# mLSTM heads in row form: denominators and norm factors as full rows, the spread of m behind the preceding head's last products

## The chip, the cores and the metric

The kernel runs on one core of a Trainium2 chip. The metric is the device time of one execution in microseconds (us). Only the engines of that one core are used: TensorE (PE; PEld is its weight load), VectorE (DVE), ScalarE (ACT), GpSimd (POOL) and SyncE (SP), which issues the weight loads.

## The reference

Two transformer blocks run one behind the other on 512 tokens of width 1024. The change touches only the mLSTM branch of the first one. The reference computes it in chunks with a running state; the kernel uses the equivalent form over the whole sequence. With F the running sum of the log forget gates, c = log i − F, M the running maximum of c (from 0) and m = F + M, each of the four heads of width 256 does:

```python
scores = (q @ k.T) / 16 * exp(c[s] - M[t])         # for s <= t, else 0
num = scores @ v
den = scores.sum(over s)
h = num / max(|den|, exp(-m))[:, None]
h = (h - mean(h)) * rsqrt(mean((h - mean(h))**2) + 1e-5)   # layer norm over the head's 256 columns
out = sigmoid(o) * h * head_g
```

Behind it come the gates with the second branch, the output projection and the rest of the two blocks.

## The kernel before

**Layout.** Activations lie transposed: features on the 128 partitions, the 512 tokens along the free axis. Every precise product is split: an fp32 operand becomes a high part in float32r (ScalarE, `xh`, `wh`) and the remainder (VectorE, `xl`, `wl`), and `mm3` issues three float32r products, high x high, high x low, low x high. A product of two fp32 operands that are not split is issued as one fp32 matmul, which shows as two records.

**Weights.** They stream as 312 units of 128x1024 through three buffers. In the plan, `("split", u)` makes SyncE fetch unit u + 3, ScalarE copy unit u to `wh` and VectorE subtract to `wl`; it stands two units ahead of TensorE's use.

**Order.** `make_plan()` writes one list of steps by hand; every engine walks through it in order and does its own part of each step, with semaphores between the engines. The projections ("pair" steps) give TensorE steady work; the steps of the heads are placed between them by tables. `MIX_AT[(u, kk)]` names the short steps that follow pair step kk of unit u. `H0.7` is step 7 of head 0's attention, `T0.7` step 7 of its norm. `GATE_AT` does the same for the gates (`Q`), the norm of the second branch (`L`) and its spatial products (`V`). The evacuation of the q and k projections (`qkev`: bias, three more taps of the convolution, silu, split) and that of the output gates (`ogev`) follow the last pair step of their units.

**Steps of a head** (before). H.0: TensorE spreads row M of head h over all partitions, by an fp32 product of `sel[:, h, :]` (4 rows, ones in row h) and `rows[:, 2, :]`, into PSUM bank 2. H.1, H.2: ScalarE takes exp(c − M), GpSimd masks the diagonal blocks. H.3: q k products. H.4: scores on VectorE. H.5, H.6: the split of the scores into `sh` and `sl`. H.7: TensorE makes the denominators as columns: for each block of 128 tokens, products of the scores (as weights) with two columns of ones, 20 in all, then the numerators, 24 products; ScalarE takes the absolute value of the 128x4 denominators, VectorE copies half of the numerator, takes the maximum with exp(−m) (which lies in `ccol` from gate step 4) and the reciprocal. T.0, T.1: the sum over the 256 columns by a product with ones; T.2: subtraction of the mean; T.3, T.4: squares; T.5: column sums of the squares (`col_sums`, four fp32 products with one column each); T.6: four VectorE operations and a Sqrt on 128x4 numbers give one factor for each token; T.7: VectorE puts them on the diagonals of a 128x512 tile; T.8: TensorE spreads these over all partitions (fp32, 512 columns); T.9: ScalarE copies the result; T.10: VectorE multiplies both halves of the head. `G` steps gate the heads' halves and add the second branch, on GpSimd for the first six.

**Gates.** `gmm` makes the gate rows, Q0 to Q2 compute log f, F, c, M and m in `rows`, Q3 transposes c and m on TensorE (eight small products), Q4 copies c and takes exp(−m) into `ccol`.

**Constants.** "mix" (GpSimd) builds `sel`; "ws" (VectorE) splits the spatial weights and scales the gates' weights, in the queue ahead of the diagonal of R, the factors of the mixing norm, whose product by TensorE stands within the next group of products.

Of the kernel before, what the change touches and what calls it, by code (L numbers as in the profile page):

```python
# [7 lines left out]
F32 = mybir.dt.float32  # L8
# [33 lines left out]
    (78, 3): "L15", (80, 1): "L16",  # L42
# [50 lines left out]
def short_steps(text):  # L93

    for w in text.split():
        name, _, seg = w.partition(".")
        c, n = name[0], name[1:]
        if c in "HT":
            yield (c, int(n), int(seg))
# [17 lines left out]
def make_plan():  # L117
# [247 lines left out]
def _build(nc, D, out, ctx):  # L365
# [50 lines left out]
    rows = sb("rows", [4, 4, 512], F32, mix)  # L416
    sel = sb("sel", [4, 4, 128], F32, mix)
# [182 lines left out]
    def three(f, p, plain, conv):  # L600
# [14 lines left out]
    mix_g = sig("s_mix_g", mix=lambda: ["sel0", "sel", "wm", "on4"])  # L615
# [6 lines left out]
                 gate=lambda i: {1: ["min", "F"], 2: ["c", "M", "m"], 4: ["cc"]}.get(i, []))  # L622
    gate_a = sig("s_gate_a", gate=lambda i: {0: ["abs", "exp", "ln"], 4: ["em"]}.get(i, []))
# [19 lines left out]
    h_p = sig("s_h_p", H=lambda h, s: {0: [(h, "M")], 3: [(h, "qk")], 7: [(h, "den"), (h, "num")]}.get(s, []))  # L643
    h_a = sig("s_h_a", H=lambda h, s: {1: [(h, "e", 0), (h, "e", 1)], 2: [(h, "e", 2), (h, "e", 3)],
                                       5: [(h, "s", 0), (h, "s", 1)], 7: [(h, "abs"), (h, "h0")]}.get(s, []))
    h_g = sig("s_h_g", H=lambda h, s: {1: [(h, 0), (h, 1)], 2: [(h, 2), (h, 3)]}.get(s, []))
    h_d = sig("s_h_d", H=lambda h, s: {4: [(h, "a", 0), (h, "a", 1)], 6: [(h, "l", 0), (h, "l", 1)],
                                       7: [(h, "h1"), (h, "max"), (h, "rec")]}.get(s, []))
    t_p = sig("s_t_p", T=lambda h, s: {1: [(h, "sum")], 5: [(h, "cs")], 8: [(h, "sp")]}.get(s, []))
    t_a = sig("s_t_a", T=lambda h, s: {3: [(h, "sq0")], 4: [(h, "sq1")], 6: [(h, "sqrt")], 9: [(h, "R")]}.get(s, []))  # L650
    t_d = sig("s_t_d", T=lambda h, s: {0: [(h, "add")], 2: [(h, "c0"), (h, "c1")], 4: [(h, "sq")],
                                       6: [(h, "v0"), (h, "v1"), (h, "rec"), (h, "v2")], 7: [(h, "diag")],
                                       10: [(h, "n0"), (h, "n1")]}.get(s, []))
# [102 lines left out]
    def _(e):  # L756
# [11 lines left out]
        for kind, *a in plan:  # L768
# [110 lines left out]
            elif kind == "gate":  # L879
                i, = a  # L880
                ra, rf = tmpm[0:4, 0, :], rows[:, 1, :]
# [7 lines left out]
                elif i == 4:  # L889
                    e.wait_ge(*gate_d.at("cc"))  # L890
                    act(ccol[:, 16:32], bank(6)[:, 16:32], ACT.Exp, scale=-1.0).then_inc(gate_a.sem, 1)
# [29 lines left out]
            elif kind == "H":  # L921
                h, s = a
                if s in (1, 2):
# [8 lines left out]
                elif s == 7:  # L932
                    e.wait_ge(*h_p.at(h, "den"))
                    act(rcs[:, h % 2, :], bank(2)[:, 0:8].rearrange("p (i z) -> p i z", z=2)[:, :, 0],
                        ACT.Abs).then_inc(h_a.sem, 1)
                    e.wait_ge(*h_p.at(h, "num"))
                    e.wait_ge(s_spill, 16)
                    act(hn[:, 2 * h, :], bank(0), ACT.Copy).then_inc(h_a.sem, 1)
            elif kind == "T":
# [145 lines left out]
    def _(e):  # L1085
# [9 lines left out]
        for kind, *a in plan:  # L1095
# [94 lines left out]
            elif kind == "ws":  # L1190
                e.wait_ge(*ws_a.at("h"))
                low(wsl[:, :], wsr[:, :], wsh[:, :]).then_inc(ws_d.sem, 1)
                for k in range(8):
                    e.tensor_scalar(wif[:, k, :], wif[:, k, :], col("gmix", k), None, ALU.mult).then_inc(ws_d.sem, 1)
            elif kind == "gmm":
                ri, rf = rows[:, 0, :], rows[:, 1, :]
# [9 lines left out]
            elif kind == "gate":  # L1206
                i, = a
                ri, rf, rM, rm = (rows[:, n, :] for n in range(4))
                if i == 1:
                    e.wait_ge(*gate_a.at("ln"))  # L1210
                    stt(rf, rf, 0.0, tmpm[0:4, 0, :], ALU.min, ALU.subtract).then_inc(gate_d.sem, 1)
# [10 lines left out]
                elif i == 4:  # L1222
                    e.wait_ge(*gate_p.at("tr"))
                    e.tensor_copy(ccol[:, 0:16], bank(6)[:, 0:16]).then_inc(gate_d.sem, 1)
            elif kind == "ln":
# [66 lines left out]
            elif kind == "H":  # L1292
# [11 lines left out]
                elif s == 7:  # L1304
                    cc = rcs[:, h % 2, :]
# [3 lines left out]
                    e.wait_ge(*h_a.at(h, "abs"))  # L1309
                    e.wait_ge(*gate_a.at("em"))  # L1310
# [905 lines left out]
```

## Time and profile before

| | us |
|---|---|
| median of three runs | 1939.83 (1939.72 to 1943.83) |
| profiled execution | 1945.08 |
| its span, first to last instruction | 1943.0 |
| TensorE busy | 1903.3 |
| VectorE busy | 1032.3 |
| ScalarE busy | 783.0 |
| GpSimd busy | 240.5 |

Times of rows are microseconds from the start of the span. The stretch in which the heads run goes from about 597 to 817 us. The busy time of TensorE includes the time in which it runs at a lower clock; the mean granted clock over the span is 0.988. A matmul's shown duration overlaps with that of the next one, so starts are to be compared. "x2" behind a row is the number of instructions merged in it.

### The profile page before, as it was taken

The numbers are of one execution on the slowest core, as the hardware profiler recorded it, in microseconds if no ns is written. First come the engines' busy times: TensorE is split into PE (matmuls) and PEld (weight loads), VectorE is DVE, ScalarE is ACT, GpSimd is POOL, SyncE is SP. The second block draws the span as 40 slices with busy tenths as digits, with TensorE's granted clock in tenths as the row PEclk, the third lists the DMA queues.
The fourth block names the chain that finished last, engine by engine and source line by source line (L and its number), as shares of the span: only waits on it lengthen the run. The fifth ranks groups of instructions, "written<-read, shape, count | busy, mean of one in ns | idle before, by whom it ended". The sixth has DMA issues, their size and how long they took to land.

```text
span 1943.0 us, 21345 instructions
## 1 busy us (share of the span) xinstructions
PE 1903.3 (98%) x8752; PEld 1571.7 (81%) x8752; DVE 1032.3 (53%) x1297; ACT 783.0 (40%) x1046; POOL 240.5 (12%) x264
## 2 busy tenths in 40 slices
PE   7999999999999999999999999999989999999997
PEld 5788888878888888888888888888877888888885
DVE  6444434347354666564444334655564877774345
ACT  4332322236443555433223222555554444443234
POOL 5000001201300111140000022100003100000212
PEclk9999999999999999999999999999989999999998
DMA  4423232342241222422222332312213232323331
GB/s 146 163 89 106 87 108 88 105 153 92 76 141 60 93 76 82 137 97 98 98 98 97 98 98 97 111 64 68 74 44 103 82 109 87 108 88 109 98 104 59
DMA packets 51074, 188.98 MB, mean 97 GB/s; under 512 B 6345, under 2 KB 6345, under 8 KB 50081
## 3 DMA queue, kind: packets, MB, share of 16 engines
q1 hardware_dynamic: 46224, 166.74, 26.0%
q0 software_dynamic: 4176, 19.83, 3.0%
q8 instruction: 69, 1.13, 0.2%
q10 hardware_dynamic: 576, 1.05, 0.1%
q14 instruction: 29, 0.23, 0.0%
HBM read 179.18 MB, written 11.03 MB: 98 GB/s over the span
## 4 chain that ended last, share of the span: by engine, by line
PE 95%; DVE 3%; ACT 1%; issue 0%; DMA 0%; DVEq 0%; ACTq 0%; POOLq 0%
PE psum L1675 95%; DVE xl L1090 1%; DVE wl L1093 1%; PE psum L2027 0%; DMA cols<-in_cols 0%; ACT at L766 0%; ACT wh L766 0%; DVE x L1087 0%; DVE az L1090 0%; DVE R L1125 0%; DVE at L1446 0%; DVE fta L1087 0%; DVE tm L1331 0%; ACT R L766 0%; DVE xl L1093 0%
## 5 line engine op out<-in xcount | busy, mean ns | idle before, releaser
L1675 PE MATMUL psum<-xh,wh 128*128 128x512 f32 x1760 | 697.1, 396 | 14.8 <-DVE xl L1090 11.6
L1675 PE MATMUL psum<-xl,wh 128*128 128x512 f32 x1760 | 687.7, 391 | 0.0
L1675 PE MATMUL psum<-xh,wl 128*128 128x512 f32 x1760 | 687.5, 391 | 0.0
L1093 DVE TENSOR_TENSOR wl<-wraw,wh 128x1024 fp32r<-128x1024 f32 (+1 forms) x313 | 405.4, 1303 | 388.1 <-ACT wh L766 387.5
L766 ACT ACTIVATE wh<-wraw 128x1024 fp32r<-128x1024 f32 (+1 forms) x313 | 325.7, 1050 | 382.1 <-PE psum L1675 380.1
L1675 PEld LDWEIGHTS psum<-xh,wh 128*128 128x128 f32 x1760 | 332.1, 189 | 94.5 <-issue 22.6
L1675 PEld LDWEIGHTS psum<-xl,wh 128*128 128x128 f32 x1760 | 332.1, 189 | 70.1 <-issue 2.9
L1675 PEld LDWEIGHTS psum<-xh,wl 128*128 128x128 f32 x1760 | 331.9, 189 | 70.1
L1539 POOL TENSOR_TENSOR ssq<-x 128x512 f32<-128x512 f32 x6 | 6.2, 1039 | 717.3 <-DVE x L1173 454.0
L1675 PE MATMUL psum<-wh,xh 128*128 128x512 f32 (+1 forms) x256 | 88.2, 344 | 0.4 <-ACT zv L766 0.4
L1675 PE MATMUL psum<-wh,xl 128*128 128x512 f32 (+1 forms) x256 | 86.0, 336 | 0.0
L1675 PE MATMUL psum<-wl,xh 128*128 128x512 f32 (+1 forms) x256 | 86.0, 336 | 0.0
L1675 PE MATMUL psum<-hha,wh 128*128 128x512 f32 x176 | 68.5, 389 | 0.0
L1675 PE MATMUL psum<-hla,wh 128*128 128x512 f32 x176 | 68.5, 389 | 0.0
L1675 PE MATMUL psum<-hha,wl 128*128 128x512 f32 x176 | 68.5, 389 | 0.0
L1675 PE MATMUL psum<-hhb,wh 128*128 128x512 f32 x176 | 68.5, 389 | 0.0
L1675 PE MATMUL psum<-hlb,wh 128*128 128x512 f32 x176 | 68.5, 389 | 0.0
L1675 PE MATMUL psum<-hhb,wl 128*128 128x512 f32 x176 | 68.5, 389 | 0.0
L1675 PE MATMUL psum<-hhc,wh 128*128 128x512 f32 x176 | 68.5, 389 | 0.0
L1675 PE MATMUL psum<-hlc,wh 128*128 128x512 f32 x176 | 68.5, 389 | 0.0
L1675 PE MATMUL psum<-hhc,wl 128*128 128x512 f32 x176 | 68.5, 389 | 0.0
L1090 DVE SCALAR_TENSOR_TENSOR ftc<-ftc,cols 128x511 f32<-128x511 f32 x88 | 64.1, 749 | 7.9 <-ACT ftc L766 6.4
(299 smaller groups left out, 2245.7 us busy)
## 6 DMA issues: line engine op xcount, KB each, us to landing
wraw<-in_w_ffn SPq DMA_DIRECT2D x87, 512.0 KB, 3.3
wraw<-in_w_down SPq DMA_DIRECT2D x44, 512.0 KB, 3.3
wraw<-in_w_up SPq DMA_DIRECT2D x44, 512.0 KB, 3.5
wraw<-in_w_qg SPq DMA_DIRECT2D x28, 512.0 KB, 3.3
wraw<-in_w_att SPq DMA_DIRECT2D x24, 512.0 KB, 3.3
wraw<-in_w_dn SPq DMA_DIRECT2D x22, 512.0 KB, 3.3
wraw<-in_w_zu SPq DMA_DIRECT2D x16, 512.0 KB, 3.3
wraw<-in_w_zv SPq DMA_DIRECT2D x8, 512.0 KB, 3.4
```

The lines of the kernel that those rows point to most:

```text
L766: return e.activation(dst, src, func, **kw)
L1090: return e.scalar_tensor_tensor(out=dst, in0=p, scalar=s, in1=q, op0=op0, op1=op1)
L1093: return e.tensor_tensor(dst, src, hi.bitcast(F32), ALU.subtract)
L1539: e.tensor_tensor(ssq[:, :], x[:, j, :], x[:, j, :], ALU.mult).then_inc(sq.sem, 1)
L1675: return e.matmul(dst, lhsT, rhs, start=start, stop=stop, skip_group_check=skip)
```

## The change

Denominators and norm factors stay rows that are alike on all partitions, so that nothing of them has to be turned from columns to rows.

- H.7: TensorE multiplies ones (128x128) with the scores, eight float32r products of 512, 384, 256 and 128 columns, which gives the denominator on all partitions. ScalarE squares it, scaled by 256e-5, into `tm(5)`; VectorE takes the maximum with 256e-5 exp(−2m), which becomes `em(h)` (in `ssg` or `R1`).
- A new step H.m: TensorE spreads row m over all partitions into bank 2, ScalarE takes exp(−2m) into `em(h)`. H0.m stands inside the second group of the v projection; the others stand 1.5 to 2 units or more ahead of their head's H.0, behind the preceding head's last products. H.0 now waits for that exponential.
- The spreads of M and m are float32r: `rowr` holds rows M and m, high parts on partitions 0 to 3 and remainders on 32 to 35, `sel` has 36 rows to match. A new gate step Q5 makes that split. "mix" and "ws" get a memset and four copies for zeros and ones.
- T.5: the sum of squares goes to all partitions by one fp32 product with ones, as in T.1. T.6: VectorE adds `em(h)`, ScalarE takes Ln and Exp(−0.5 ·). T.7 multiplies both halves. T.8 to T.10 are gone.
- The gates' transposes of m and their exponential are gone; gate rows move to `mg`.

```diff
-    (78, 3): "L15", (80, 1): "L16",
+    (78, 3): "L15 Q5", (80, 1): "L16",
...
+    (103, 1): "H0.7", (103, 2): "T0.0 H1.m", (103, 3): "T0.1", (104, 0): "T0.2", (105, 3): "T0.3 T0.4",
...
-    (109, 1): "H1.6", (110, 0): "T0.8", (110, 1): "H1.7 T0.9", (110, 3): "T0.10 G0 G1 T1.0", (111, 0): "T1.1",
-    (111, 1): "T1.2 T1.3", (111, 2): "T1.4", (111, 3): "T1.5", (112, 0): "T1.6", (114, 0): "H2.0 T1.7",
-    (114, 1): "H2.1 H2.2", (115, 2): "H2.3 T1.8 H2.4", (115, 3): "T1.9 H2.5", (116, 2): "T1.10 G2",
+    (109, 1): "H1.6", (110, 1): "H1.7", (110, 3): "G0 G1 T1.0", (111, 0): "T1.1",
+    (111, 1): "T1.2 T1.3", (111, 2): "T1.4 H2.m", (111, 3): "T1.5", (112, 0): "T1.6",
+    (114, 0): "H2.0 T1.7", (114, 1): "H2.1 H2.2", (115, 2): "H2.3 H2.4", (115, 3): "H2.5", (116, 2): "G2",
...
-    (119, 2): "T2.4", (119, 3): "T2.5", (120, 0): "T2.6", (122, 0): "H3.0 T2.7", (122, 1): "H3.1 H3.2",
+    (119, 2): "T2.4 H3.m", (119, 3): "T2.5", (120, 0): "T2.6", (122, 0): "H3.0 T2.7",
...
-        tgroup("v", c, 94 + 4 * c)
+        tgroup("v", c, 94 + 4 * c, {(1, 0, 3): (("H", 0, "m"),)} if c else None)
...
# ScalarE
+                if s == "m":
+                    e.wait_ge(*h_p.at(h, "m"))
+                    if h >= 2:
+                        e.wait_ge(*t_d.at(h - 2, "u"))
+                    act(em(h), bank(2), ACT.Exp, scale=-2.0).then_inc(h_a.sem, 1)
...
-                    act(rcs[:, h % 2, :], bank(2)[:, 0:8].rearrange("p (i z) -> p i z", z=2)[:, :, 0],
-                        ACT.Abs).then_inc(h_a.sem, 1)
+                    if h:
+                        e.wait_ge(*t_d.at(h - 1, "n1"))
+                    act(tm(5), bank(2), ACT.Square, scale=256e-5 ** 0.5).then_inc(h_a.sem, 1)
...
-                    act(c2, c2, ACT.Sqrt, bias=eps5[:, 0:1]).then_inc(t_a.sem, 1)
-                elif s == 9:
-                    e.wait_ge(*t_p.at(h, "sp"))
-                    act(tm(4), bank(7), ACT.Copy).then_inc(t_a.sem, 1)
+                    e.wait_ge(*t_d.at(h, "u"))
+                    act(tm(5), tm(5), ACT.Ln, scale=1.0 / 256).then_inc(t_a.sem, 1)
+                    e.wait_ge(*t_a.at(h, "ln"))
+                    act(tm(5), tm(5), ACT.Exp, scale=-0.5).then_inc(t_a.sem, 1)
...
# VectorE
+                e.wait_ge(*mix_g.at("zero"))
+                sel2 = sel[:, :, :].rearrange("p h t -> p (h t)")
+                e.tensor_copy(sel2, mg[0:36, 4, :]).then_inc(sel_d.sem, 1)
+                e.tensor_copy(rowr[:, :, :], mg[0:36, 4:6, :]).then_inc(sel_d.sem, 1)
+                e.wait_ge(*sel_d.at("zero"))
+                e.tensor_copy(sel2[0:4, :], mg[0:4, 3, :]).then_inc(sel_d.sem, 1)
+                e.tensor_copy(sel2[32:36, :], mg[0:4, 3, :]).then_inc(sel_d.sem, 1)
...
-                    e.tensor_tensor(cc, cc, ccol[:, 16:32].rearrange("p (i h) -> p i h", h=4)[:, :, h],
-                                    ALU.max).then_inc(h_d.sem, 1)
-                    e.wait_ge(*h_d.at(h, "max"))
-                    e.reciprocal(cc, cc).then_inc(h_d.sem, 1)
+                    e.wait_ge(*h_a.at(h, "em"))
+                    e.wait_ge(*h_a.at(h, "d"))
+                    stt(em(h), em(h), 256e-5, tm(5), ALU.mult, ALU.max).then_inc(h_d.sem, 1)
...
-                    stt(c2, bD[:, 0:4], 1.0 / 256, cc, ALU.mult, ALU.mult).then_inc(t_d.sem, 1)
...
+                    stt(tm(5), em(h), 3.0e38, bD, ALU.min, ALU.add).then_inc(t_d.sem, 1)
...
-                    e.tensor_tensor(quad(t4), eye4, wide(c2), ALU.mult).then_inc(t_d.sem, 1)
...
# TensorE
+                if s == "m":
                     if h:
-                        e.wait_ge(*h_a.at(h - 1, "abs"))
+                        e.wait_ge(*h_a.at(h - 1, "d"))
...
-                    mm(bank(2), sel[:, h, :], rows[:, 2, :]).then_inc(h_p.sem, 1)
+                    mm(bank(2), sel[:, h, :], rowr[:, 1, :]).then_inc(h_p.sem, 1)
+                elif s == 0:
+                    e.wait_ge(*h_a.at(h, "em"))
+                    mm(bank(2), sel[:, h, :], rowr[:, 0, :]).then_inc(h_p.sem, 1)
...
-                    for i in range(4):
-                        for j in range(i + 1):
-                            r = slice(OFF[j] + 128 * (i - j), OFF[j] + 128 * (i - j) + 128)
-                            mm(bD[:, 2 * i:2 * i + 2], sh[:, r], onesr[:, 0:2], j == 0, False)
-                            t = mm(bD[:, 2 * i:2 * i + 2], sl[:, r], onesr[:, 0:2], False, j == i)
+                    for j in range(4):
+                        r = slice(OFF[j], OFF[j] + 512 - 128 * j)
+                        mm(bank(2)[:, 128 * j:512], onesr[:, :], sh[:, r], j == 0, False)
+                        t = mm(bank(2)[:, 128 * j:512], onesr[:, :], sl[:, r], False, j == 3)
...
-                    col_sums(bank(7), tm(4)).then_inc(t_p.sem, 1)
-                elif s == 8:
-                    e.wait_ge(*t_d.at(h, "diag"))
                     mm(bank(7), ones[:, :], tm(4)).then_inc(t_p.sem, 1)
```

## Rows read from the trace of the kernel before

**Rows 1.** The page's first part: busy us, share of the span, instructions.

```profile
PE 1903.3 (98%) x8752; PEld 1571.7 (81%) x8752; DVE 1032.3 (53%) x1297; ACT 783.0 (40%) x1046; POOL 240.5 (12%) x264
```

**Rows 2.** Waits of TensorE, 560 to 830 us: total, times, longest.

```profile
PE psum L1675 <- DVE tm L1331: 0.6, 1, 0.6
```

**Rows 3.** TensorE by stretches: length, busy (instructions), granted clock, DMA share, GB/s.

```profile
612.02:615.40 3.38, 3.38 (x11) 0.50 0.00 0
...
721.25:724.65 3.40, 3.40 (x12) 0.50 0.44 177
...
779.25:782.70 3.45, 3.45 (x11) 0.51 0.70 209
```

**Rows 4.** Timeline of TensorE, head 0's step 7: start, us, instruction.

```profile
608.85 0.39 PE L1675 MATMUL psum<-xh,wl 128*128 128x512 f32 x1
609.08 0.17 PE L1675 MATMUL psum<-onesr,sh 128*128 128x2 f32 x1
...
611.22 0.49 PE L1675 MATMUL psum<-sh,vh 128*128 128x512 f32 x1
...
616.63 0.45 PE L1675 MATMUL psum<-xh,wh 128*128 128x512 f32 x1
```

**Rows 5.** Timeline of TensorE, head 1's numerators and what follows.

```profile
664.75 0.48 PE L1675 MATMUL psum<-sh,vh 128*128 128x512 f32 x1
...
668.59 0.45 PE L1675 MATMUL psum<-xh,wh 128*128 128x512 f32 x1
```

**Rows 6.** Timeline of TensorE around step T0.1.

```profile
619.21 0.39 PE L1675 MATMUL psum<-xh,wl 128*128 128x512 f32 x1
619.44 1.02 PE L1675 MATMUL psum<-tm,ones 128*128 128x512 f32 x2
...
620.76 0.40 PE L1675 MATMUL psum<-xh,wl 128*128 128x512 f32 x1
```

**Rows 7.** Timeline of TensorE on both sides of step T2.5.

```profile
737.32 0.39 PE L1675 MATMUL psum<-xh,wl 128*128 128x512 f32 x1
...
738.92 0.40 PE L1675 MATMUL psum<-xh,wl 128*128 128x512 f32 x1
```

**Rows 8.** Timeline of TensorE around step H0.0.

```profile
596.96 0.39 PE L1675 MATMUL psum<-xh,wl 128*128 128x512 f32 x1
597.27 1.12 PE L1675 MATMUL psum<-rows,sel 4*128 4x512 f32 x2
...
598.90 0.39 PE L1675 MATMUL psum<-xh,wl 128*128 128x512 f32 x1
```

**Rows 9.** Timeline of TensorE, one 64-row group of the attention stage.

```profile
1342.81 0.40 PE L1675 MATMUL psum<-xh,wl 128*128 128x512 f32 x1
1343.14 2.18 PE L1675 MATMUL psum<-aq 64*128 64x512 f32 x12
...
1345.82 0.40 PE L1675 MATMUL psum<-xh,wl 128*128 128x512 f32 x1
```

**Rows 10.** Timelines of VectorE and TensorE around the mixing norm's R.

```profile
408.91 0.69 DVE L1128 TENSOR_TENSOR R<-ident,rc 128x512 f32<-128x512 f32 x1
...
411.27 1.02 PE L1675 MATMUL psum<-R,ones 128*128 128x512 f32 x2
...
433.03 0.48 DVE L1203 TENSOR_SCALAR rows<-rows,bif 4x512 f32<-4x512 f32 x1
```

**Rows 11.** Timelines: a dependent ScalarE pair, then T1.6 to H2.3.

```profile
437.54 1.29 ACT L766 ACTIVATE tmpm<-tmpm 4x512 f32<-4x512 f32 x2
...
688.31 0.15 DVE L1090 SCALAR_TENSOR_TENSOR rcs<-psum,rcs 128x4 f32<-128x4 f32 x1
...
688.90 1.05 ACT L766 ACTIVATE wh<-wraw 128x1024 fp32r<-128x1024 f32 x1
...
698.60 0.69 DVE L1093 TENSOR_TENSOR qk<-tmpm,qk 128x512 fp32r<-128x512 f32 x1 [0.76 <-ACT qk L766]
...
701.17 1.07 PE L1675 MATMUL psum<-qk 128*128 128x512 f32 x4
```

More of the change, by code:

```diff
@@ L98, in short_steps @@
         if c in "HT":
-            yield (c, int(n), int(seg))
+            yield (c, int(n), seg if seg == "m" else int(seg))
         elif c == "S":
@@ L415, in _build @@
     vl = sb("vl", [128, 4, 1024], F32R, mix)
-    rows = sb("rows", [4, 4, 512], F32, mix)
-    sel = sb("sel", [4, 4, 128], F32, mix)
+    rows = sb("rows", [4, 2, 512], F32, mix)
+    rowr = sb("rowr", [36, 2, 512], F32R, mix)
+    sel = sb("sel", [36, 4, 128], F32R, mix)
     tmpm = sb("tmpm", [128, 4, 512], F32, mix)
@@ L497, in tm, with em @@
         return tmpm[:, i, :] if i < 4 else tm2[:, i - 4, :]
+    def em(h):
+        return (R1 if h % 2 else ssg)[:, :]
     def quad(ap):
@@ L621, in _build @@
     gate_d = sig("s_gate_d", gmm=lambda: ["i0", "f0", "i", "f"],
-                 gate=lambda i: {1: ["min", "F"], 2: ["c", "M", "m"], 4: ["cc"]}.get(i, []))
-    gate_a = sig("s_gate_a", gate=lambda i: {0: ["abs", "exp", "ln"], 4: ["em"]}.get(i, []))
+                 gate=lambda i: {1: ["min", "F"], 2: ["c", "M", "m"], 4: ["cc"], 5: ["rl"]}.get(i, []))
+    gate_a = sig("s_gate_a", gate=lambda i: {0: ["abs", "exp", "ln"], 5: ["rh"]}.get(i, []))
     ln_d = sig("s_ln_d", ln=lambda i: {0: [("ag", 0)], 1: [("ag", 1)], 2: [("ag", 2)], 3: [("ag", 3)], 4: ["rec"],
@@ L880, in _ @@
                 i, = a
-                ra, rf = tmpm[0:4, 0, :], rows[:, 1, :]
+                ra, rf = mg[0:4, 1, :], mg[0:4, 0, :]
                 if i == 0:
@@ L888, in _ @@
                     act(ra, ra, ACT.Ln, bias=1.0).then_inc(gate_a.sem, 1)
-                elif i == 4:
-                    e.wait_ge(*gate_d.at("cc"))
-                    act(ccol[:, 16:32], bank(6)[:, 16:32], ACT.Exp, scale=-1.0).then_inc(gate_a.sem, 1)
+                elif i == 5:
+                    e.wait_ge(*gate_d.at("m"))
+                    e.wait_ge(*sel_d.at("rowz"))
+                    act(rowr[0:4, :, :], rows[:, :, :], ACT.Copy).then_inc(gate_a.sem, 1)
             elif kind == "zuev":
@@ L1207, in _ @@
                 i, = a
-                ri, rf, rM, rm = (rows[:, n, :] for n in range(4))
+                ri, rf, rM, rm = mg[0:4, 2, :], mg[0:4, 0, :], rows[:, 0, :], rows[:, 1, :]
                 if i == 1:
                     e.wait_ge(*gate_a.at("ln"))
-                    stt(rf, rf, 0.0, tmpm[0:4, 0, :], ALU.min, ALU.subtract).then_inc(gate_d.sem, 1)
+                    stt(rf, rf, 0.0, mg[0:4, 1, :], ALU.min, ALU.subtract).then_inc(gate_d.sem, 1)
                     e.wait_ge(*gate_d.at("min"))
@@ L1224, in _ @@
                     e.tensor_copy(ccol[:, 0:16], bank(6)[:, 0:16]).then_inc(gate_d.sem, 1)
+                elif i == 5:
+                    e.wait_ge(*gate_a.at("rh"))
+                    low(rowr[32:36, :, :], rows[:, :, :], rowr[0:4, :, :]).then_inc(gate_d.sem, 1)
             elif kind == "ln":
@@ L1566, in _ @@
                 e.dma_start(bif[:, :], D["bif"]).then_inc(s_bif, 16)
-                e.memset(sel[:, :, :], 1.0).then_inc(mix_g.sem, 1)
+                sel0 = mg[0:4, 3, :].rearrange("p (h t) -> p h t", h=4)
+                e.memset(sel0, 1.0).then_inc(mix_g.sem, 1)
                 e.wait_ge(*mix_g.at("sel0"))
-                e.affine_select(out=sel[:, :, :], in_=sel[:, :, :], pattern=[[-1, 4], [0, 128]],
+                e.affine_select(out=sel0, in_=sel0, pattern=[[-1, 4], [0, 128]],
                                 compare_op=ALU.is_equal, fill=0.0, base=0,
                                 channel_multiplier=1).then_inc(mix_g.sem, 1)
+                e.memset(mg[0:36, 4:6, :], 0.0).then_inc(mix_g.sem, 1)
                 e.dma_start(wif[:, :, :], D["wif"]).then_inc(s_misc, 16)
@@ L1735, in _ @@
                         else:
-                            e.wait_ge(*t_a.at(3, "R"))
+                            e.wait_ge(*t_d.at(3, "u"))
                     elif st == "ao":
@@ L1831, in _ @@
             elif kind == "gate" and a[0] == 3:
-                e.wait_ge(*gate_d.at("m"))
+                e.wait_ge(*gate_d.at("c"))
                 for i in range(4):
                     r = slice(128 * i, 128 * i + 128)
-                    e.transpose(bank(6)[:, 16 + 4 * i:20 + 4 * i], rows[:, 3, r], ident[0:4, 0:4])
-                    t = e.transpose(bank(6)[:, 4 * i:4 * i + 4], rows[:, 0, r], ident[0:4, 0:4])
+                    t = e.transpose(bank(6)[:, 4 * i:4 * i + 4], mg[0:4, 2, r], ident[0:4, 0:4])
                 t.then_inc(gate_p.sem, 1)
@@ L1846, in _ @@
                 else:
-                    e.wait_ge(*gate_a.at("em"))
+                    e.wait_ge(*gate_d.at("cc"))
                 for n in range(4):
```

48 lines of the change are left out of this document (16 added, 32 removed), and 9 rows, old and new, of the table MIX_AT.

## The prediction

> **What bounds the kernel now.** I read the page first. TensorE is busy for 1903.3 of 1943.0 us [rows 1], so a microsecond saved elsewhere is worth nothing unless TensorE was waiting for it, and a microsecond taken out of TensorE's own queue is worth a microsecond as long as nothing else becomes late. The second view is TensorE's waits inside the mixing stage, where the heads run (560 to 830 us): a single wait of 0.6 us [rows 2]. So the stage is bound by what TensorE is given to do and by the clock at which it does it. The third view is therefore the timeline of TensorE around each step the diff touches. There the reader should look at starts, not durations: the matmuls overlap, and a 512-column product of the projections takes 0.227 us from its start to the next one's. The cost of an inserted step is the distance between two such products on either side of it, less 0.68 us for the three ordinary products in between. The fourth view is the granted clock in short stretches.
>
> **The clock.** Behind the denominators of heads 0, 2 and 3 the granted clock is about 0.50 for 3.4 us: TensorE runs at 1.2 instead of 2.4 GHz [rows 3]. Head 0's numerator products take from 611.22 to 616.63, 5.41 us [rows 4]; the same 24 products of head 1, at full clock, take from 664.75 to 668.59, 3.84 us [rows 5]. A fall costs 1.57 us, three of them 4.7 us. What TensorE did just before each fall is the 20 products with two columns; in head 1 it did the same and kept its clock, so that stretch makes a fall likely, not certain. The Trainium skill speaks against me here: "TensorE: Matmul & The Clock Gate", "Why this matters for your kernels", ties drops in the middle of a kernel to idle gaps between bursts of matmuls. The trace shows no idle gap there. By that page denser denominators need not bring the clock back, and 4.7 us would drop out of the sum.
>
> **The change on TensorE, for each head.**
> *Denominator.* Before: from 608.85 (last product ahead) to 611.22, less 0.23, is 2.14 us for 20 products, 0.11 us each [rows 4]. After: eight products, two for each width of 512, 384, 256 and 128. Head 1's numerator has six of each width in 3.84 us [rows 5], so one set of four widths takes 0.64 and the new denominator 1.28 us. Saved 0.86, over four heads 3.4 us.
> *Last spread (T.8).* It goes altogether. Its twin T.1, an fp32 product of 512 columns, takes 620.76 − 619.21 − 0.68 = 0.87 us [rows 6]. Saved 3.5 us.
> *Column sums (T.5).* Before, 738.92 − 737.32 − 0.68 = 0.92 us [rows 7]; after, one product like T.1, 0.87. Saved 0.2 us.
> *Spreads of M and m.* Before there was one, fp32 over 4 rows: 598.90 − 596.96 − 0.68 = 1.26 us [rows 8]. After there are two in float32r over 36 rows. No row shows 36 rows. The nearest is the attention stage's group over 64 rows: 1345.82 − 1342.81 − 0.68 = 2.33 us for three sets of widths, which at 0.64 are 1.92 [rows 9]. The other 0.41 us is going into and out of the smaller row count (the 4-row spread shows as much beyond T.1's 0.87). So each new spread costs 0.23 + 0.41 = 0.64, both 1.28: over four heads a loss of 0.1 us. From below they cost 0.23 each (no drain), which would save another 3.3 us; from above, 1.26 each, a loss of 5.0. I take 0.64, because the 64-row group has the same type. The Trainium skill, "TensorEngine Tiling (Array Packing)", "Key Properties", says that a change of tiling mode drains TensorE, which is a reason against splitting one spread into two; the trace agrees, with 0.41 us.
> *Gate transposes.* Four of eight go, at about 0.06 us of TensorE each: 0.2 us. 0.11 us, the pace of the small denominator products, bounds it at 0.4.
> *The 0.6 us wait.* It is head 1's T.5 waiting for the sum of squares [rows 2]. Now H2.m, 0.64 us, stands ahead of T1.5 in TensorE's queue, while on VectorE the multiplies of T0.10 have left the queue ahead of that chain. The wait should vanish: 0.6 us.
> Sum 3.4 + 3.5 + 0.2 − 0.1 + 0.2 + 0.6 = 7.8 us.
>
> **What it adds elsewhere.** *Constants.* VectorE gets four copies in "ws", ahead of the diagonal R of the mixing norm, which ends at 409.60; TensorE takes it at 411.27 [rows 10], a margin of 1.7 us. A single-source operation on 4x512 takes 0.48 us [rows 10]; three such copies and one of twice the length are 1.9 to 2.3 us. TensorE then waits 0.2 to 0.6, I take 0.4 us. If the copies ran at the 0.69 us of the R multiply it would be 3 x 0.69 + 1.23 = 3.3 us and the wait 1.6; if they pipelined closely, none. GpSimd's extra memset only delays loads that are used later. The added gate step Q5 (ScalarE copy, VectorE subtraction of 1024 columns, about 1 us each) replaces a ScalarE exponential with its table load and lies in VectorE's idle time behind the gate; nothing on TensorE wants it before H0.m, more than 100 us later.
> *T.6.* Four tiny VectorE operations and a 0.30 us Sqrt become a full-width VectorE operation (about 0.7) and Ln and Exp one behind the other; such a pair took 1.29 us in the gates [rows 11]. Queued behind them on ScalarE in heads 1 and 2 is the copy to wh of the next weights, behind that VectorE's wl, and behind that qkev(h+1, 1). wh starts at 688.90 now; it would start at 688.31 + 0.7 + 1.29 plus handover, 690.35: 1.45 us later. The last half of q and k is now ready at 698.60 + 0.69 = 699.29 and TensorE starts H2.3 at 701.17 [rows 11], a margin of 1.9 us. It loses 1.45, and 0.6 more because the cheaper H2.0 brings TensorE there sooner. That is a wait of about 0.2 us, twice: 0.4 us (0 to 2.9, where no margin covers it). The weights themselves have a margin of more than 3 us.
> *H.m.* TensorE waits there for ScalarE's Square of the denominator, queued behind nothing new, and H.0 waits for the Exp of the spread m. H0.m comes some 14 us ahead of H0.0, H1.m some 20; the price is nothing. Two more table loads (1.28 us each) fall on ScalarE in H2.m and H3.m, but they run beside TensorE's next pair step (1.36 us) and VectorE's first multiply (0.7 us), and only then does qkev want ScalarE. Uncovered they would cost 1.9 us each.
> *H.7 and T.0.* The full-width maximum on VectorE (0.7 against 0.33 us) delays T.0 by 0.4 us. H1.m and two pair steps, 3.3 us, cover head 0's T.1; later heads have more.
> Loss 0.4 + 0.4 = 0.8. Without the clock the change saves 7.8 − 0.8 = 7.0 us, with it 11.7 us.
>
> **The base.** The profiled execution took 1945.08 us, of which 1943.0 is its span. The sum gives 1933.4 us for one like it. The median of the plain runs is 5.25 us lower, and the same saving gives 1928.1 us. Plain runs may hold fewer than three falls, since falls are not certain; each one fewer takes 1.6 us from the gain.
>
> **The rivals.**
> *A: the clock does not return,* or the plain runs had hardly any falls. For: head 1, and the page named above. Against: three of four falls stand right behind the sparse products, and the equally narrow 128-column products of the numerators bring none. 1939.83 − 7.0 = 1932.8 us.
> *B: a wait takes the place of the removed work.* Candidates are H2.3 and H3.3 behind the T.6 pair, and the constants ahead of R. For: the margins of 1.9 and 1.7 us are all but used. Against: they have to be used up first. At their upper prices (2.9 + 1.6 instead of 0.8), 3.7 us are lost: 1931.8 us.
> *C: spreads of 36 rows without a drain.* Gain 11.7 + 3.3: 1924.8 us. Against: 4 rows and 64 rows both show it.
> *D, slower:* the drains of the eight 36-row spreads bring the clock down instead, at each of them, while the old falls stay. 8 x 1.57 = 12.6 us against 7.0 saved: 1945.4 us. It decides from five falls on. Against: the clock stays at full through the four 4-row spreads and the 64-row group of [rows 9].
> *E: nothing to be seen,* two or three such falls: about 1938 us.
>
> **How the numbers follow.** My forecast 0.60; A 0.19; B 0.11; C 0.05; D 0.02; E 0.03. A change under 0.2%, 3.9 us, can hardly be told from none. Faster 0.95, within 0.2% 0.03, slower 0.02. The range reaches down past C toward four falls removed (1.6 more) and up past A with part of B's waits: 1923.5 to 1933.5 us.
>
> **What would show it.** Right: granted clock 1.00 throughout the four head stretches; eight onesr products in about 1.3 us; each spread 0.64; no T.8; TensorE's busy time about 12 us lower. A wait before the qk products of heads 2 and 3, or before the R product near 411 us, is B. Wrong: falls at clock 0.50 behind the new spreads or numerators, or spreads that run as slowly as fp32.

## The result, and the profile after

The changed kernel takes 1936.26 us (median of 18 runs, 1934.43 to 1940.69). The kernel before, timed beside it, takes 1940.71 us (18 runs, 1936.73 to 1944.34). The ratio is 0.998, 95% interval 0.9974 to 0.9987: 4.45 us faster, where the forecast had 11.7. The sign was right and the time lies above the range.

The profiled execution of after took 1937.08 us, its span is 1935.1. The page's first part, as [rows 1] for before:

```profile
PE 1891.2 (98%) x8668; PEld 1559.2 (81%) x8668; DVE 1031.2 (53%) x1282; ACT 790.3 (41%) x1051; POOL 242.2 (13%) x265
```

TensorE is busy 12.1 us less, almost exactly the "about 12 us" of the forecast. The profiled executions differ by only 8.0 us, so some 4 us came back as idle time. The second view is TensorE's waits, 380 to 830 us (total, times, longest):

```profile
PE psum L1686 <- DVE qk L1105: 2.7, 2, 1.3
PE psum L1686 <- DVE sl L1105: 2.0, 1, 2.0
PE psum L1686 <- ACT zv L773: 0.4, 1, 0.4
PE psum L1686 <- DVE vl L1102: 0.3, 1, 0.3
```

The wait of [rows 2] is gone. Three others have come: for `qk` before H2.3 and H3.3, for `sl` before H1.7, for `vl` in H0.3. The 0.4 us at `zv` were there before.

The third view is the granted clock, in stretches that cover the numerators of the four heads (columns as in [rows 3], with the busy time and instructions of PE, PEld, DVE, ACT and POOL behind the length):

```profile
608.00:620.00 12.00, 12.00 (x61) 9.70 (x60) 4.63 (x7) 3.01 (x5) 0.00 (x0) 1.00 0.13 44
655.00:672.00 17.00, 14.96 (x75) 12.54 (x74) 12.68 (x14) 7.93 (x11) 6.67 (x5) 1.00 0.33 109
712.00:726.00 14.00, 14.00 (x73) 12.14 (x72) 9.85 (x11) 4.28 (x6) 5.28 (x4) 1.00 0.30 95
770.00:785.00 15.00, 15.00 (x77) 12.97 (x76) 9.19 (x11) 3.62 (x6) 5.19 (x5) 1.00 0.43 133
```

The three falls to half clock are gone, as forecast.

**The steps on TensorE.** Its timeline at head 0's denominators and at the spread H0.0 of after, to be read by starts:

```profile
598.12 0.39 PE L1686 MATMUL psum<-xh,wl 128*128 128x512 f32 x1
598.44 0.50 PE L1686 MATMUL psum<-rowr,sel 36*128 36x512 f32 x1
...
599.42 0.39 PE L1686 MATMUL psum<-xh,wl 128*128 128x512 f32 x1
...
610.13 0.39 PE L1686 MATMUL psum<-sh,onesr 128*128 128x512 f32 x1
...
611.34 0.44 PE L1686 MATMUL psum<-sh,vh 128*128 128x512 f32 x1
```

The denominator takes 611.34 − 610.13 = 1.21 us (forecast 1.28; before 2.14 [rows 4]). The spread costs 599.42 − 598.12 − 0.68 = 0.62 us (forecast 0.64).

**Where it came back.** The timeline of TensorE in after, ahead of H1.7 and of H2.3:

```profile
659.96 0.39 PE L1686 MATMUL psum<-xh,wl 128*128 128x512 f32 x1
662.38 0.50 PE L1686 MATMUL psum<-sh,onesr 128*128 128x512 f32 x1 [2.04 <-DVE sl L1105]
...
699.02 0.39 PE L1686 MATMUL psum<-xh,wl 128*128 128x512 f32 x1
700.74 4.30 PE L1686 MATMUL psum<-qk 128*128 128x512 f32 x24 [1.33 <-DVE qk L1105]
704.87 0.40 PE L1686 MATMUL psum<-xh,wh 128*128 128x512 f32 x1
```

From start to start the wait at H1.7 is 662.38 − 659.96 − 0.23 = 2.19 us, the one at H2.3 1.49 us, and the one at H3.3 is its twin (1.48). The products behind a wait also start more slowly: the 24 of H2.3 need 704.87 − 700.74 = 4.13 us, and 3.81 in before, where nothing is waited for: they start at 701.17 [rows 11], and T1.8's spread follows at 704.98.

```profile
704.98 1.02 PE L1675 MATMUL psum<-tm,ones 128*128 128x512 f32 x2
```

So each of these two waits costs 1.8 us.

**A measure that leaves the rest out.** From the start of the gates' first product (`x,wif`) to the first product of the output projection (`hhb,wh`) before takes 1093.38 − 424.51 = 668.87 us and after 1087.06 − 425.32 = 661.74: 7.13 us less. I call this the stretch below. Outside it the two kernels are the same but for the constants, yet the clock falls there at places that differ from execution to execution (near 20 us, 1230 to 1300 us and 1430 to 1450 us), so a difference between two traces is read from the stretch.

### The profile page after: what moved, and what is told of

Read it like the earlier page. It is cut to its first block, busy times and chain, and to the rows that moved or that the text cites. A ratio compares the mean times of both kernels' runs of the same rounds, so it can differ in the third digit from the quotient of the medians.

```text
span 1935.1 us, 21174 instructions
## 1 busy us (share of the span) xinstructions
PE 1891.2 (98%) x8668; PEld 1559.2 (81%) x8668; DVE 1031.2 (53%) x1282; ACT 790.3 (41%) x1051; POOL 242.2 (13%) x265
## 4 chain that ended last, share of the span: by engine, by line
PE 92%; DVE 4%; ACT 2%; issue 1%; DMA 0%; DVEq 0%; ACTq 0%; POOLq 0%
PE psum L1686 92%; DVE tmpm L1102 1%; DVE wl L1105 1%; DVE xl L1102 0%; ACT wh L773 0%; ACT tmpm L773 0%; PE psum L2035 0%; DMA cols<-in_cols 0%; DVE x L1099 0%; ACT at L773 0%; ACT L769 0%; DVE az L1102 0%; DVE R L1137 0%; DVE at L1455 0%; ACT tm L773 0%
## 5 line engine op out<-in xcount | busy, mean ns | idle before, releaser
L1686 PE MATMUL psum<-xh,wh 128*128 128x512 f32 x1760 | 697.2, 396 | 14.6 <-DVE xl L1102 11.9
```

The source lines that it names most:

```text
L1686: return e.matmul(dst, lhsT, rhs, start=start, stop=stop, skip_group_check=skip)
```

## The experiments

Each variant was timed beside the kernel before, whose median was 1939.4 to 1939.7 us; the ratios are to it. The changed kernel itself was not timed beside its variants, so a difference between their medians and its 1936.26 us is less certain than the ratios. The diffs of tables show the changed entries alone, taken out of longer lines.

**1. The products before the falls, spread out** (`interleaved_den`, on the kernel before). The 20 two-column products of H.7 are not issued in a row but one ahead of each of the first 20 numerator products. Nothing is added or removed.

```diff
-                    for i in range(4):
-                        for j in range(i + 1):
-                            r = slice(OFF[j] + 128 * (i - j), OFF[j] + 128 * (i - j) + 128)
-                            mm(bD[:, 2 * i:2 * i + 2], sh[:, r], onesr[:, 0:2], j == 0, False)
-                            t = mm(bD[:, 2 * i:2 * i + 2], sl[:, r], onesr[:, 0:2], False, j == i)
...
+                    dens = [(i, j, b) for i in range(4) for j in range(i + 1) for b in (sh, sl)]
+                    for n in range(24):
+                        j, c, which = n // 6, n % 6 // 3, n % 3
+                        if n < 20:
+                            i, jj, buf = dens[n]
+                            q = slice(OFF[jj] + 128 * (i - jj), OFF[jj] + 128 * (i - jj) + 128)
+                            t = mm(bD[:, 2 * i:2 * i + 2], buf[:, q], onesr[:, 0:2], jj == 0 and buf is sh,
+                                   jj == i and buf is sl)
...
+                        t = mm(psum[:, 512 * c + 128 * j:512 * c + 512], (vh, vh, vl)[which][:, j, w],
+                               (sh, sl, sh)[which][:, r], j == 0 and which == 0, j == 3 and which == 2)
```

> The kernel before, with its 20 two-column denominator products dealt out among the 24 numerator products, one ahead of each; the same work in another order. Theory 1 (the stretch of sparse products brings the clock down): the granted clock of the head stretch stays at 1.00, TensorE's work is unchanged, and each fall that an execution of the kernel before had behind the denominators (three in its profiled one, 1.57 us each) is gone: 0 to 4.7 us faster, some 2.5 to 4 on the median. Theory 2 (the falls come from the mixture of small numerator products or from chance): falls of clock 0.50 stay in the head stretch and the median moves by less than 1 us.

> The kernel before with the interleaved denominators, a second trace. If the stretch of sparse products is the cause of the falls there: none between 590 and 830 us again.

Stretches of head 0, 2 and 3, first of `interleaved_den`:

```profile
605.00:620.00 15.00, 15.00 (x83) 12.83 (x82) 6.51 (x10) 4.30 (x7) 0.00 (x0) 1.00 0.10 35
712.00:730.00 18.00, 18.00 (x96) 15.32 (x95) 11.08 (x14) 4.00 (x6) 6.53 (x5) 1.00 0.28 99
771.00:790.00 19.00, 19.00 (x101) 16.13 (x100) 10.82 (x14) 5.24 (x8) 5.58 (x5) 1.00 0.34 111
```

then of the kernel before, traced again (`before_third`):

```profile
605.00:620.00 15.00, 15.00 (x76) 13.02 (x75) 5.01 (x8) 2.75 (x6) 0.00 (x0) 0.89 0.09 35
...
771.00:790.00 19.00, 19.00 (x94) 16.18 (x93) 10.88 (x14) 4.39 (x7) 7.17 (x6) 0.91 0.33 111
```

The falls are gone, in both traces of this kernel, and the stretch is shorter by 4.74 and 4.75 us: three times the 1.57 us that the forecast gave a fall. The timed result is another matter: 1937.91 us (1936.07 to 1942.55, 11 runs) against 1939.69, ratio 0.9995 (0.9987 to 1.0004). Not told from no change, and certainly not 4.7 us. Of Theory 1 the falls came true, its 2.5 to 4 us on the median did not. `interleaved_again`, one run, took 1937.71.

**2. How regular the falls are** (`before_again`, `before_third`, `before_fourth`, `after_again`: the two kernels unchanged, traced again).

> The kernel before once more, for its trace: how many falls of the clock stand behind the denominators in another execution. If three of four were the rule (as my prediction took it): three, and about 1943 us. If the profiled execution was an unlucky one: none to two, and about 1939 us.

> The kernel before, a third trace. The first showed three falls of the clock behind the denominators and 1945.08 us, the second two and 1941.2. If the number of falls there is what sets an execution's place in the spread of the kernel before: one or two, and 1938 to 1941 us.

> The kernel before, a fourth trace, for the same question: one or two falls behind the denominators, 1938 to 1941 us.

> The changed kernel once more, for its trace: no falls of the clock between 590 and 830 us, and the same four waits of TensorE there (0.3, 2.0, 1.3 and 1.3 us). If a fall stands there, the dense denominators have not removed the cause.

The four traces of before have 3, 2, 3 and 3 falls, never at head 1: 11 of 16 heads. Their stretches differ from the first one's by −1.50 (the one with two falls), −0.03 and +0.07 us, and they took 1941.2, 1940.83 and 1940.85 us. The third and the fourth were expected to have one or two falls; they have three, and still took less than 1941 us. The first profile of before, 1945.08 us, was thus 4 us above its own repeats, and about 3 of these lie in a fall outside the heads that the three repeats don't have, here its window:

```profile
1243.48:1250.31 6.83, 6.83 (x18) 4.98 (x17) 5.46 (x8) 6.66 (x9) 1.60 (x5) 0.50 0.45 190
```

`after_again` took 1936.97 us; its stretch is 5.57 shorter than that of before, 1.56 less than after's, because one fall is in it, right behind the wait for `sl`:

```profile
660.00:668.00 8.00, 7.04 (x34) 6.33 (x35) 5.24 (x6) 2.79 (x5) 5.29 (x5) 0.79 0.25 71
```

No fall had been expected there: "If a fall stands there, the dense denominators have not removed the cause." They have removed one cause. What stands ahead of this fall is the new wait of 2.0 us, and the three traces with dense denominators and without that wait (experiments 5 and 6) have no fall in the heads.

**3. The trigger put back into after** (`sparse_too`). The old 20 products stand ahead of the eight new ones, into the same bank, which the new ones overwrite. It is work added and nothing else.

```diff
+                    for i in range(4):
+                        for j in range(i + 1):
+                            r = slice(OFF[j] + 128 * (i - j), OFF[j] + 128 * (i - j) + 128)
+                            mm(bank(2)[:, 2 * i:2 * i + 2], sh[:, r], onesr[:, 0:2], j == 0, False)
+                            mm(bank(2)[:, 2 * i:2 * i + 2], sl[:, r], onesr[:, 0:2], False, j == i)
                     for j in range(4):
                         mm(bank(2)[:, 128 * j:512], onesr[:, :], sh[:, r], j == 0, False)
```

> The changed kernel, with the old 20 two-column products issued once more ahead of the eight dense ones (their result is overwritten). Work alone: 4 x 2.14 = 8.6 us, less what hides in the waits for sl, q and k: the 2.0 us of head 1 is not hidden, since the products stand behind the same wait. Theory 1: falls come back behind the sparse stretches, two to four of 1.57 us, so 1936.3 + 8.6 + 3 to 6 = 1948 to 1951 us. Theory 2: no falls, 1945 us.

1950.83 us (1948.25 to 1954.15, 5 runs), ratio to before 1.0057 (1.0044 to 1.007). The falls are back, behind heads 1, 2 and 3; the stretch is 15.37 us longer than after's. Four times 2.14 us are the work, 8.6; the other 6.8 are the clock. Here the times show it as well: 14.6 us more than after, 6.0 beyond the work. At head 1 the products stand behind the wait of 2.0 us for `sl`, so of the falls only those of heads 2 and 3 are put down to the products alone. A window of TensorE behind head 1's products in this kernel:

```profile
663.00:675.00 12.00, 10.43 (x51) 9.76 (x52) 5.71 (x5) 2.77 (x4) 5.76 (x5) 0.72 0.23 75
```

**4. The wait for qk** (`late_factors`, on after). T1.6 and T2.6, with their table loads, Ln and Exp, are moved behind the evacuation of q and k instead of ahead of it; T1.7 and T2.7 follow.

```diff
-    (111, 3): "T1.5", (112, 0): "T1.6",
-    (114, 0): "H2.0 T1.7", (114, 1): "H2.1 H2.2", (115, 2): "H2.3 H2.4",
+    (111, 3): "T1.5",
+    (114, 0): "H2.0", (114, 1): "H2.1 H2.2 T1.6", (115, 2): "H2.3 H2.4 T1.7",
... (the same for T2.6 and T2.7)
```

> The changed kernel, with T1.6 and T2.6 behind H2.2 and H3.2 (same activation table) and T1.7 and T2.7 behind H2.4 and H3.4. Theory 1 (the Ln and Exp of T.6, full width and one behind the other, hold up wh, wl and so q and k of the next head): both waits of 1.3 us before the q k products go, and two pairs of table loads with them: 2.7 us faster than the changed kernel, 1933.6. Theory 2 (the q and k evacuation is late for another reason, VectorE's load): the waits stay and the time is that of the changed kernel, 1936.3.

1931.06 us (1930.9 to 1938.6, 5 runs), ratio 0.9965 (0.9951 to 0.9978). The two waits for `qk` are gone from the list, nothing takes their place, and the other three stand as in after; the first line of TensorE's waits:

```profile
PE psum L1686 <- DVE sl L1105: 2.0, 1, 2.0
```

Its stretch is 2.07 us shorter than after's with one fall in it, 3.64 without: 1.82 for each wait, as start to start plus the slower restart gave. The median lies 5.2 us below after's, more than these 3.6 and than the 2.7 expected; with five runs that spread over 7.7 us, and after not timed beside them, the rest is not explained.

Why the wait is so long: ScalarE in after, then VectorE.

```profile
687.80 1.28 ACT L769 ACT_TABLE_LOAD   x1 [1.88 <-DVE tm L1102]
689.09 1.30 ACT L773 ACTIVATE tm<-tm 128x512 f32<-128x512 f32 x2
690.29 1.04 ACT L773 ACTIVATE wh<-wraw 128x1024 fp32r<-128x1024 f32 x1
```

```profile
687.10 0.68 DVE L1102 SCALAR_TENSOR_TENSOR tm<-R,psum 128x512 f32<-128x512 f32 x1
691.37 1.23 DVE L1105 TENSOR_TENSOR wl<-wraw,wh 128x1024 fp32r<-128x1024 f32 x1 [3.60 <-ACT wh L773]
...
699.99 0.69 DVE L1105 TENSOR_TENSOR qk<-tmpm,qk 128x512 fp32r<-128x512 f32 x1 [0.76 <-ACT qk L773]
```

and ScalarE in before at the same step, ahead of its copy to wh [rows 11]:

```profile
687.16 1.28 ACT L766 ACT_TABLE_LOAD   x1
688.70 0.30 ACT L766 ACTIVATE rcs<-rcs,eps 128x4 f32<-128x4 f32 x1 [0.26 <-DVE rcs L1087]
```

Both kernels load a table here. In before the load is over when VectorE's numbers come; in after it starts behind VectorE's addition (687.10 + 0.70 = 687.80). In the code, T6 first waits for the addition, and `act()` issues the load of Ln's and Exp's table behind that wait. So wh starts 0.70 + 1.28 + 1.21 = 3.19 us behind the start of T1.6 on VectorE, against 688.90 − 688.31 = 0.59 in before [rows 11]: 2.60 us later, where the forecast had 1.45. In absolute times the forecast (690.35) and the trace (690.29) agree, but by luck: T1.6 as a whole begins 1.21 us earlier in after (687.10 for 688.31). The margin of 1.88 us loses 2.60, and 0.71 on TensorE's side (699.02 + 0.23 = 699.25 for 701.17, less the common 1.21; forecast 0.6): a wait of 1.43, and the trace shows 1.49.

**5. The wait for sl** (`t07_behind_sl`, on after). Two neighbours change places: T0.7, the multiplies of head 0, goes behind H1.6, the split of head 1's scores.

```diff
-    (109, 0): "T0.7", (109, 1): "H1.6",
+    (109, 1): "H1.6 T0.7",
```

> The changed kernel, with T0.7 moved from ahead of H1.6 to right behind it, nothing else. Theory 1 (VectorE's two multiplies of T0.7 stand ahead of head 1's sl, and finishing them starts GpSimd's gating beside it, which stretches the 768-column sl from about 0.96 to 2.0 us): of the 2.0 us wait before the denominators of head 1 some 1.9 go, and the qk waits stay: 1934.2. Theory 2 (sl is late because sh is, behind the Ln and Exp of T0.6): the wait shrinks by the multiplies' 1.3 us at most and 0.7 or more stays: 1935.

1934.72 us (1933.37 to 1937.22, 11 runs), ratio 0.9976 (0.9967 to 0.9985); the stretch is 2.27 us shorter than after's, and the wait for `sl` is off the list. The swap takes 1.28 us of multiplies from ahead of `sl` and 1.07 us from `sl` itself; what is left is a margin of 0.12 us (`sl` ready at 658.51, TensorE at 658.63). First after:

```profile
657.36 1.23 DVE L1105 TENSOR_TENSOR wl<-wraw,wh 128x1024 fp32r<-128x1024 f32 x1 [0.98 <-ACT wh L773]
658.50 1.28 DVE L1099 TENSOR_TENSOR x<-x,tm 128x512 f32<-128x512 f32 x2
659.71 2.62 DVE L1105 TENSOR_TENSOR sl<-att,sh 128x512 fp32r<-128x512 f32 x2
```

and GpSimd in after:

```profile
659.94 1.57 POOL L1626 TENSOR_TENSOR tm<-tm,x 128x512 f32<-128x512 f32 x1 [15.81 <-DVE x L1099]
661.59 1.89 POOL L1629 TENSOR_TENSOR x<-tm 128x512 f32<-128x512 f32 x1
```

then VectorE in `t07_behind_sl`:

```profile
656.96 1.55 DVE L1105 TENSOR_TENSOR sl<-att,sh 128x512 fp32r<-128x512 f32 x2
658.43 1.28 DVE L1099 TENSOR_TENSOR x<-x,tm 128x512 f32<-128x512 f32 x2
```

The sum for this wait is made like that of T1.6, from the start of T0.6 on VectorE (652.42 in before, 650.88 in after, so everything is 1.54 us earlier). In before `sl` is ready at 658.04 + 1.55 = 659.59 and TensorE comes at 662.60: a margin of 3.01. In after `sl` is ready at 662.33, 2.74 later, and against T0.6 4.28 later. The parts: 2.61 in the chain wh, wl that T0.6 now holds up (`wl` at 657.36 for 656.29), again with a table load behind the wait; 0.59 since two multiplies (1.28 us) stand ahead of `sl` where one diagonal tile of 0.69 stood; and 1.07 since `sl` itself takes 2.62 us for 1.55. TensorE comes 0.87 earlier, without T0.8's spread. 4.28 + 0.87 − 3.01 = 2.14 us, and 2.19 are in the trace. The 1.07 come from the neighbour: the multiplies release GpSimd's first gating product, which had waited for `x` and now runs beside `sl`. The Trainium skill, "SBUF — State Buffer", "Who interferes with whom", says that a VectorE instruction with two SBUF inputs contends with a GpSimd instruction that reads SBUF, and that the port pair they share is locked exclusively. The trace agrees. The two pieces of `sl` in after, by form (busy us, mean ns):

```profile
L1105 DVE TENSOR_TENSOR sl<-att,sh 128x768 fp32r<-128x768 f32 x1 | 2.0, 2018 | 0.0
L1105 DVE TENSOR_TENSOR sl<-att,sh 128x512 fp32r<-128x512 f32 x1 | 0.7, 685 | 0.0
```

The smaller piece starts at 659.71, ahead of GpSimd's product, and takes 0.69 us, as in `t07_behind_sl` (0.68). The larger one starts at 660.31, within that product (659.94 to 661.51), and takes 2.02 us for 0.95.

**6. All waits moved away** (`all_moved`). Both edits above, and three small ones: H0.3 goes behind one more pair step (it waited for `vl`), T0.6 from behind H1.4 to behind H1.5, and the four copies of the constants from "ws" to the start of the gates' step.

```diff
-    (102, 1): "H0.1 H0.2 H0.3", (102, 2): "H0.4",
+    (102, 1): "H0.1 H0.2", (102, 2): "H0.3 H0.4",
...
-    (107, 3): "H1.4 T0.6", (108, 3): "H1.5",
+    (107, 3): "H1.4", (108, 3): "H1.5 T0.6",
...
-    sel_d = sig("s_sel_d", ws=
+    sel_d = sig("s_sel_d", gmm=
```

> As late_factors, and also: T0.6 behind H1.5, T0.7 behind H1.6, so that head 1's sl is no longer behind the two multiplies and no GpSimd operation starts beside it; H0.3 one pair step later; the four copies of the constants from ws into gmm. Theory 1 (all of what the change gives back is in the four kinds of waits, 2.0 + 2.7 + 0.3 us, and 0.2 at R): no wait of TensorE between 404 and 830 us; 5.2 us faster than the changed kernel, 1931.1. Rival: something else takes their place, since VectorE and ScalarE are near their limit there: 1933 to 1936.

> all_moved once more, five rounds and a second trace: 1928.6 us as before, no wait of TensorE between 410 and 830 us and no fall of the clock there.

1928.6 us (1927.84 to 1930.49, 5 runs), ratio 0.9944 (0.9931 to 0.9958), and again 1927.53 (1927.31 to 1932.86, 5 runs), 0.9948 (0.9934 to 0.9961). Of the waits only one is left:

```profile
PE psum L1685 <- ACT zv L773: 0.4, 1, 0.4
```

The stretch is 13.64 us shorter than that of before (again 13.60), with the clock at full throughout the four heads in both traces. This is the best version, about 0.55% below the kernel before. It is 2.5 us faster than expected; of the 7.7 us below after's median the stretch and the R product account for 6.7. That it comes near 1928.1 us, the forecast for the change as it stood, is chance: more work is removed than forecast, nothing is lost to waits, and the clock gives less.

**7. The place of H.m** (`m_at_head`, on `all_moved`). H1.m to H3.m are moved from behind the preceding head's last products to their own head's H.0.

```diff
-    (103, 2): "T0.0 H1.m", (106, 0): "H1.0", (111, 2): "T1.4 H2.m",
-    (114, 0): "H2.0", (119, 2): "T2.4 H3.m", (122, 0): "H3.0",
+    (103, 2): "T0.0", (106, 0): "H1.m H1.0", (111, 2): "T1.4",
+    (114, 0): "H2.m H2.0", (119, 2): "T2.4", (122, 0): "H3.m H3.0",
```

> As all_moved, but H1.m, H2.m and H3.m directly ahead of H1.0, H2.0 and H3.0 instead of behind the preceding head's last products. Theory 1 (the early place is what hides ScalarE's table load and Exp between the two spreads): at each of the three TensorE waits about 2 us for em (table load 1.28, Exp 0.6, handover), so 5 to 6.5 us slower than all_moved: 1934 to 1935. Theory 2 (ScalarE has the table already or the wait is absorbed by a later margin): within 1 us of all_moved, 1928.6 to 1929.6.

1963.27 us (1962.1 to 1964.01, 4 runs), ratio to before 1.0124 (1.011 to 1.0138). Both theories were far too low. TensorE's waits:

```profile
PE psum L1685 <- ACT R L773: 18.4, 2, 9.8
PE psum L1685 <- ACT ssg L773: 8.6, 1, 8.6
```

TensorE's and ScalarE's timelines at head 1 show why:

```profile
630.37 0.50 PE L1685 MATMUL psum<-rowr,sel 36*128 36x512 f32 x1
640.63 0.79 PE L1685 MATMUL psum<-rowr,sel 36*128 36x512 f32 x1 [9.77 <-ACT R L773]
```

```profile
629.96 1.52 ACT L773 ACTIVATE tmpm<-tmpm,cols 128x512 f32<-128x512 f32 x2 [3.27 <-DVE tmpm L1099]
...
637.63 1.04 ACT L773 ACTIVATE wh<-wraw 128x1024 fp32r<-128x1024 f32 x1
638.69 1.28 ACT L769 ACT_TABLE_LOAD   x1
639.98 0.60 ACT L773 ACTIVATE R<-psum 128x512 f32<-128x512 f32 x1
```

The exponential of m is 0.6 us of work, but ScalarE takes it in the order of the plan, behind the whole evacuation of q and k, and H.0 waits for it. The idle time brings the clock down as well, for 10.2 us each time; head 1's window stands for the three:

```profile
634.00:645.00 11.00, 4.37 (x11) 3.18 (x12) 4.54 (x6) 7.36 (x12) 1.66 (x5) 0.53 0.16 53
```

Against `all_moved` the place is worth 1963.27 − 1928.6 = 34.7 us. About 27 us of it are the waits; the rest is mostly the clock. It is what the title of the change speaks of. The forecast had put the price of H.m at nothing where it stands, and after has no wait there.

## Why the prediction was right or wrong

**The work removed: right, a little low.** `all_moved` has no wait and no fall in the heads. Its 13.6 us less 4.7 for the clock are 8.9 us of work, where the forecast summed 7.8. Of the 1.1 more, 0.3 are the denominators (1.21 for 1.28, four times) and 0.2 the spreads; the rest I can't place. The drain at 36 rows is there, 0.39 us beyond a plain product: rival C is out, and so is D, no fall came with the eight spreads of after.

**"it would start at 688.31 + 0.7 + 1.29 plus handover": the step that failed.** The table load of 1.28 us is missing in it. [rows 11] show the pair of Ln and Exp without one, but in the trace of before a load stands directly ahead of that pair, which ran at 437.54:

```profile
436.24 1.28 ACT L762 ACT_TABLE_LOAD   x1
```

The forecast counted such loads for H2.m and H3.m and not here; the load that stands at T1.6 in before, for Sqrt, is hidden ahead of its wait. With 1.28 us more the text's own sum gives 0.17 + 1.28 = 1.45 us for each wait, 2.9 for both, its upper end. Measured are 1.49 each and 0.32 for the slower restart, 3.6 in all: 3.2 more than the 0.4 taken. It is rival B's mechanism. That moving T.6 takes both waits away is shown (`late_factors`); that the load is the missing term is read from the trace, no run leaves out the load alone. The saving on TensorE's side, 0.6, was right to 0.1.

**A wait that was not on the list: H1.7 for sl.** The same missing load strikes at T0.6, but the forecast priced T.6 for heads 1 and 2 alone, and did not follow VectorE's queue in head 0's norm past `wl` to head 1's `sl`. It asked of the multiplies of T0.10 only what their leaving gains, not what stands behind T0.7's at their new place nor whom they release. The price is 2.3 us. A smaller one is H0.3 at `vl`: 600.78 − 600.11 − 0.23 = 0.44 us and 0.1 for the restart, since the cheaper H0.0 brings TensorE there sooner. Together the waits gave back 3.64 + 2.27 + 0.54 = 6.45 us; the stretch of `all_moved` against after's says 6.51.

**The constants: right in kind.** The four copies run from 408.29 to 410.12, 1.8 us (forecast 1.9 to 2.3), and delayed the R product by 0.2 us (forecast 0.4).

**The clock: mechanism right, its worth on the median wrong.** In the stretches the falls behind the denominators and their price are as forecast, 3 x 1.57 = 4.7 us where an execution has three. In the medians the 4.7 us are not there. Without the clock, after should gain 8.9 − 6.5 − 0.2 = 2.2 us; measured are 4.45 (2.5 to 5.0 by the interval), so about 2 us are left for the clock. `interleaved_den`, which changes nothing else, gives 1.8 by the medians and 0.9 by the means (1938.78 of 11 runs against 1939.67 of 15). The mean granted clock over the span says the same. Three falls of 3.4 us at half clock are 3 x 3.4 x 0.5 / 1940 = 0.0026 of it, but it averages 0.9901 over the 11 runs of `interleaved_den` and 0.9903 over the 15 of before. So over the whole execution the clock did not come back as it did in the heads. Whether before has fewer falls in timed runs, or whether a fall saved in the heads tends to come elsewhere, the runs don't tell: only profiled executions show the places. Those are too few. Outside the heads, beyond what all traces share, the four of before have 6.8, 0, 0 and 0 us at half clock, the two with interleaved denominators 3.4 and 0, the six of after, `late_factors`, `t07_behind_sl` and `all_moved` 0 to 13.7. The two with 13.7 (`late_factors` and `t07_behind_sl`) are the slowest execution of their kernel. This stays open. The forecast named the case ("plain runs may hold fewer than three falls") and gave it too little weight, after one profile that was itself 4 us slower than its repeats. Its argument from the "equally narrow 128-column products" compared unequal things: those have 128 columns, the products before the falls two.

**The account.** Of the 7.25 us between forecast (11.7) and result (4.45), 3.2 are the waits for `qk`, 2.3 the one for `sl`, 0.5 the one for `vl` and 2.5 the clock; 1.1 more work removed and 0.2 less at the constants stand against them. The clock's part is what remains of the measured time, so it carries the scatter of the medians.

**By the rivals.** The result is none of them alone: it is B, above its upper price for `qk` and at a place more, together with about half of A. Rival E has the nearest number (about 1938 us; its two falls would give 1936.0 by its own prices), but not the mechanism: no fall stands behind a new spread.

## What to carry to other kernels

Take a margin between two engines from a step that both have behind them, follow the whole chain from there on both sides, down to the last instruction queued behind the one that grew and to whomever its result releases: here four such waits paid back 6.5 of 13.6 us, and moving seven short steps and four copies in the order got it all again. When a step gets another function on ScalarE, ask where its table load is issued: ahead of the step's wait it is hidden, behind it it is 1.28 us of the chain (issuing it ahead, without moving the step, was not tried). And take a gain of the clock from several profiles of the kernel before, and from the medians of a variant that changes the clock alone, before it goes into a sum.

## What the runs showed of the hardware

**Falls without idle time.** The clock fell to 1.2 GHz, for 3.4 us, behind 20 products of two columns in a row (2.14 us, no idle gap), in 11 of 16 such places of four traces (heads 0, 2 and 3 in 11 of 12, head 1 in none of four). With the same products between wide ones it fell at none of the eight places of two traces:

```profile
607.91 0.17 PE L1675 MATMUL psum<-onesr,sh 128*128 128x2 f32 x1
607.93 0.48 PE L1675 MATMUL psum<-sh,vh 128*128 128x512 f32 x1
```

Behind a single idle wait of 2.0 us it fell in two of the three traces that have that wait with the dense products (`after_again` and `late_factors`, not after), and within each of the three waits of 8.6 to 9.8 us in `m_at_head`. The Trainium skill, "TensorE: Matmul & The Clock Gate", "Why this matters for your kernels", ties drops in the middle of a kernel to idle gaps between bursts. The long waits agree. The falls behind the two-column products have no gap, and there the measurement decides: TensorE went from one product to the next, and the clock fell.

**A wait costs more than its length.** The 24 products of q and k took 3.81 us when they followed other work directly, 4.13 behind a wait of 1.3 us and 3.90 behind one of 0.3 us, at a granted clock of 1.00 in the windows around them. The eight denominator products took 1.21 us directly and 1.34 behind the wait of 2.0 us in after.

**Two engines at one memory.** The same two pieces of `sl` took 1.55 us alone and 2.62 us beside GpSimd's product; all of the difference is in the piece that started behind GpSimd's.
